# Prompt attention: scores as 64-row products in the two halves of the array, heads inside query tiles

## What is computed

```python
def diff_attention(q, k, v, q_pos, k_pos, lam):
    s = jnp.einsum('bqhcd,bkhcd->bhcqk', q.astype(F32), k.astype(F32)) * (A_HEAD_DIM ** -0.5)
    visible = (k_pos[None, :] // CHUNK) <= (q_pos[:, None] // CHUNK)
    s = jnp.where(visible, s, -jnp.inf)
    p = jax.nn.softmax(s, axis=-1)
    w = p[:, :, 0] - lam * p[:, :, 1]
    return jnp.einsum('bhqk,bkhe->bqhe', w, v.astype(F32))
```

## Time and profile before

| | |
|---|---|
| median of three timed runs | 3132.71 us |
| lowest and highest | 3132.15 and 3134.53 us |
| profiled execution, first to last instruction | 3130.3 us |
| prompt attention in it, first score to last output copy | 1095.0 to 1613.9 us |
| busy in the whole span: PE, DVE, ACT, POOL | 91%, 49%, 33%, 14% |

### The profile page before, as it was taken

One profiled execution on the slowest core, in us unless ns is written; L12 is line 12 of the kernel. 1 busy time (PEld: TensorE's weight loads), 2 busy tenths in 40 slices (PEclk: granted clock), 3 DMA queues, 4 the chain that ended last, 5 costly groups with the idle time before them and its releaser, 6 DMA issues. The chain is left out here.

```text
span 3130.3 us, 41253 instructions
## 1 busy us (share of the span) xinstructions
PE 2847.6 (91%) x12609; PEld 1768.4 (56%) x12610; DVE 1540.2 (49%) x3077; ACT 1025.9 (33%) x2269; POOL 430.3 (14%) x684
## 2 busy tenths in 40 slices
PE   8999999999999688989877999599999999999960
PEld 6777777777777546556555555344444444444430
DVE  2555556555555677877743555422323233232327
ACT  2333333333342255656634555101011111101108
POOL 2111111111111111212210010101110101111000
PEclk9999999999999899999988999699999999999985
DMA  6000100000010240000033222287776557675658
GB/s 233 34 24 24 40 30 23 35 32 27 23 39 25 81 153 9 10 10 8 10 100 110 92 84 86 89 317 271 260 261 234 200 216 269 229 284 191 233 189 307
DMA packets 180197, 382.80 MB, mean 122 GB/s; under 512 B 13571, under 2 KB 51203, under 8 KB 177937
## 3 DMA queue, kind: packets, MB, share of 16 engines
q1 hardware_dynamic: 165808, 333.76, 29.6%
q0 software_dynamic: 14304, 48.08, 4.0%
HBM read 310.73 MB, written 71.08 MB: 122 GB/s over the span
## 5 line engine op out<-in xcount | busy, mean ns | idle before, releaser
L656 PE MATMUL z_psum<-w_in_sb,hT 128*128 128x512 f32 x1088 | 480.5, 592 | 0.0
L650 PE MATMUL z_psum<-hT,w_in_sb 128*128 128x128 f32 x3264 | 374.4, 276 | 0.8 <-ACT hT L326 0.8
L650 PEld LDWEIGHTS z_psum<-hT,w_in_sb 128*128 128x128 f32 x3264 | 370.2, 193 | 1.7 <-ACT hT L326 1.2
L1016 PE MATMUL score_psum<-att_k,q_by_map 128*128 (+3 forms) x640 | 280.2, 565 | 64.9 <-ACT probs L877 29.4
L1970 PE MATMUL gate_psum<-w_gate_sb,block_rows_T 128*128 x720 | 321.2, 599 | 5.6 <-SPq L1802 3.7
L656 PEld LDWEIGHTS z_psum<-w_in_sb,hT 128*128 128x128 f32 x1088 | 200.5, 190 | 221.0 <-issue 221.0
L1994 PE MATMUL down_psum<-w_down_sb,hidden_T 128*128 x720 | 323.7, 592 | 0.9 <-ACT hidden_T L1876 0.9
L1974 PE MATMUL up_psum<-w_up_sb,block_rows_T 128*128 x720 | 316.3, 592 | 0.0
L877 ACT ACTIVATE probs<-score_psum,neg_max 128x512 f32<-128x512 f32 (+3 forms) x320 | 196.4, 621 | 149.5 <-DVE neg_max L945 148.6
L1679 PE MATMUL y_psum<-w_out_sb,mix_T 128*128 128x512 f32 x544 | 243.6, 601 | 0.9 <-DVE mix_T L1536 0.9
L1974 PEld LDWEIGHTS up_psum<-w_up_sb,block_rows_T 128*128 128x128 f32 x720 | 136.8, 190 | 172.2 <-issue 172.2
(11 more groups left out here) (311 smaller groups left out, 3653.7 us busy)
## 6 DMA issues: line engine op xcount, KB each, us to landing
w_gate_sb<-in_w_e_gate SPq DMA_DIRECT2D x32, 2048.0 KB
w_up_sb<-in_w_e_up SPq DMA_DIRECT2D x32, 2048.0 KB, 15.2
w_down_sb<-in_w_e_down SPq DMA_DIRECT2D x32, 2048.0 KB, 18.2
expert_rows<-scratch_moe SPq DMA_DIRECT2D x17, 1024.0 KB, 8.2
w_in_sb<-in_w_in SPq DMA_DIRECT2D x7, 2048.0 KB, 19.6
scratch_z<-z_ring SPq DMA_DIRECT2D x34, 256.0 KB, 2.0
scratch_h<-h SPq DMA_DIRECT2D x17, 512.0 KB, 2.6
x_tile<-in_x_prompt SPq DMA_DIRECT2D x16, 512.0 KB
```

The lines of the kernel that those rows point to most:

```text
L650: mm = pe.matmul(out[:, hd * P:(hd + 1) * P], w[:, c, col:col + P], hT[:, u, c, :], start=(c == 0), stop=(c == DC - 1))
L656: mm = pe.matmul(out[:, :], hT[:, u, c, :], w[:, c, g * HW:(g + 1) * HW], start=(c == 0), stop=(c == DC - 1))
L1016: mm = pe.matmul(sps[(BASE[i] + s) % 2][:, c, 0:kw * P], qz[:, i % 2, c, :], k[:, k0:k0 + kw, bass.ds(h * P, P)], start=True, stop=True)
```

## The change

Four things change together.

- The scale of 1/8 moves from `maps` into the copy that takes q out of PSUM in `project`; `q_by_map` and `maps` are gone, and in `attend_sample` two scalings become copies.
- A map's scores are a product over that map's 64 partitions alone, map 0 on rows 0 to 63 of the array, map 1 on rows 64 to 127. A segment of 512 columns stays one product per map; map 0's product stands ahead of map 1's.
- The order is one list of 64 units, tile by tile and in a tile head by head, all written out. The lags stay: `turn` and `weighted` three units later, `out_row` four.
- q, k and v of a group of tiles come in with all heads, one semaphore for the three; outputs of four heads are stored together, 512 columns. PE's wait for its own transposes is gone, ACT waits on `w_ok` and `tg_ps` in its place. Map 0's probabilities keep four buffers, map 1's have two.

```diff
-                    nc.scalar.copy(z[:, j, :], zps[0][:, :]).then_inc(z_act, 1)
+                    nc.scalar.activation(z[:, j, :], zps[0][:, :], ACT.Copy, scale=Q_SCALE if j == QA else 1.0).then_inc(z_act, 1)
...
+    UNITS = [(i, h) for i in range(NT) for h in range(HEADS)]
+    NU = len(UNITS)
+    SEGS = [seg_of(i) for i, h in UNITS]
+    FIRST = [sum(len(s) for s in SEGS[:u]) for u in range(NU + 1)]
+    GROUPS = [0, 1, 2, 4, 8, NT]
+    LAG = 3
...
+                for buf, src in ((k, dr["z"][KT]), (q, dr["z"][QA]), (v, vp)):
+                    sp.dma_start(buf[:, c, :], src[c].rearrange("t p d -> p t d")).then_inc(t_in[g], 16)
+            for i in range(NT):
+                sp.wait_ge(o_ok, HEADS * (i + 1))
+                sp.dma_start(dr["att"][i], o[:, i % 2, :]).then_inc(att_out[i % 2], 16)
...
+            def expo(u, s):
                 if s == 0:
-                    wait(act, wt_tile, h * NT + i - 3)
+                    wait(act, w_ok, FIRST[max(u - 1, 0)])
+                    wait(act, tg_ps, FIRST[max(u - 3, 0)])
...
-            def maps(h, i):
-                wait_loaded(dve, q_in, q_rest, h, i)
-                wait(dve, s_ps, h * PER_HEAD + (BASE[i - 1] if i else -NSEG[NT - 1]))
-                for c in range(2):
-                    r = slice(64 * c, 64 * c + 64)
-                    ins = ts(qz[r, i % 2, c, :], q[r, i, bass.ds(h * P, P)], scale, None, ALU.mult)
-                ins.then_inc(qz_ok, 1)
...
-            def scores(h, i, s):
-                if s == 0:
-                    pe.wait_ge(qz_ok, h * NT + i + 1)
-                    wait_loaded(pe, k_in, k_rest, h, i)
-                pe.wait_ge(e_ok, n + 1)
-                for c in range(2):
-                    mm = pe.matmul(sps[(BASE[i] + s) % 2][:, c, 0:kw * P], qz[:, i % 2, c, :],
-                                   k[:, k0:k0 + kw, bass.ds(h * P, P)], start=True, stop=True)
+            def scores(u, s):
+                if h == 0 and s == 0 and i in GROUPS:
+                    pe.wait_ge(t_in[GROUPS.index(i)], 48)
+                wait(pe, e_ok, n - 1)
+                for c in range(2):
+                    r = slice(64 * c, 64 * c + 64)
+                    mm = pe.matmul(sps[n % 2][:, c, 0:kw * P], q[r, i, head(u)], k[r, k0:k0 + kw, head(u)], start=True, stop=True)
                 mm.then_inc(s_ps, 1)
...
-                if s == NSEG[i] - 1:
-                    pe.wait_ge(tg_ps, n + 1)
-                    pe.sem_inc(wt_tile, 1)
...
+            for u in range(NU + LAG):
+                cur, old = count(u), count(u - LAG)
+                for s in range(max(cur, old)):
+                    if s < old:
+                        turn(u - LAG, s)
+                    if s < cur:
+                        scores(u, s)
+                    if 0 < s < old:
+                        weighted(u - LAG, s - 1)
+                if old:
+                    weighted(u - LAG, old - 1)
```

More of the change, by code:

```diff
@@ L24 @@
 HIDDEN = -1e30
+Q_SCALE = 64 ** -0.5
 DEC_B = 8
@@ L757, in attend, with count, cols, head @@
     ident = consts["ident"]
[L758 to L794, removed]
+    UNITS = [(i, h) for i in range(NT) for h in range(HEADS)]
[4 more added lines that the diff above has]
+    LAG = 3
+    def count(u):
+        return len(SEGS[u]) if 0 <= u < NU else 0
+    def cols(u, s):
+        k0, kw = SEGS[u][s]
+        return slice(k0 * P, (k0 + kw) * P)
+    def head(u):
+        h = UNITS[u][1]
+        return slice(h * P, (h + 1) * P)
     with ExitStack() as ctx:
@@ L886, in factor, with copy_T @@
+                ins.then_inc(e_ok, 1)
+            def factor(u):
+                act.wait_ge(nM_ok, u + 1)
+                for c in range(2):
+                    ins = nc.scalar.activation(fac[:, u % 2, c, 0:count(u)], nmax[:, u % 2, c, 0:count(u)], ACT.Exp,
+                                               scale=-1.0, bias=tot[:, u % 2, c:c + 1])
                 ins.then_inc(ef_ok, 1)
-            def copy_T(h, i, s):
-                n = h * PER_HEAD + BASE[i] + s
-                kw = seg_of(i)[s][1]
+            def copy_T(u, s):
+                n = FIRST[u] + s
+                kw = SEGS[u][s][1]
@@ L986, in step, with out_row @@
+            def out_row(u):
+                i, h = UNITS[u]
+                dve.wait_ge(pv, FIRST[u + 1])
+                if h == 0:
+                    wait(dve, att_out[i % 2], 16 * (i // 2))
+                nc.vector.tensor_copy(o[:, i % 2, head(u)], ops[u % 2][:, 0:P]).then_inc(o_ok, 1)
+            for u in range(NU + LAG + 1):
+                cur, mid = count(u), count(u - 1)
                 if mid:
-                    factors(h1, i1)
+                    factors(u - 1)
                 if cur:
-                    seg_max(h, i, 0)
+                    seg_max(u, 0)
@@ new lines, in turn, with weighted @@
+            def turn(u, s):
+                n = FIRST[u] + s
+                k0, kw = SEGS[u][s]
+                pe.wait_ge(w_ok, n + 1)
+                wait(pe, wt_sb, n - 1)
+                for b in range(kw):
+                    mm = pe.transpose(tps[n % 2][:, b * P:(b + 1) * P], p0[:, u % 4, (k0 + b) * P:(k0 + b + 1) * P], ident[:, :])
+                mm.then_inc(tg_ps, 1)
+            def weighted(u, s):
+                n = FIRST[u] + s
+                k0, kw = SEGS[u][s]
+                if s == 0:
+                    wait(pe, o_ok, u - 1)
@@ L1046, in weighted @@
                 mm.then_inc(pv, 1)
-            def step(h, i):
-                cur = NSEG[i] if i < NT else 0
-                h3, i3, old = tile_before(h, i, 3)
+            for u in range(NU + LAG):
+                cur, old = count(u), count(u - LAG)
                 for s in range(max(cur, old)):
                     if s < old:
-                        turn(h3, i3, s)
+                        turn(u - LAG, s)
                     if s < cur:
-                        scores(h, i, s)
+                        scores(u, s)
```

176 lines of the change are left out of this document (55 added, 121 removed).

## The result

The changed kernel took 3061.89 us (median of 4 runs, 3059.75 to 3064.2) against 3133.62 us before (4 runs, 3132.15 to 3134.7): a ratio of 0.9772, 95% interval 0.976 to 0.9784.

A forecast was written before the change was run, and what follows sets the result against it. No engine was full in prompt attention; a ring of waits among ACT, DVE and PE bound it. Terms -4.4 - 36.8 + 8 + 0.5 = -33 us on 3130.3 gave 3097.5; medians lie 2.4 higher, so 3100, range 3078 to 3124.

The forecast's parts named there:

- Scores: Prompt attention's score products on 64 rows: three passes' time instead of four, plus two shape changes of 0.15 us; -4.4 us.
- The rival that had them side by side: Score products of both maps overlap fully, pass by pass: 3086 us, or 3076 with free shape changes; chance 0.20.
- S: Time a whole segment's scores occupy TensorE in prompt attention: 1.71 us before, forecast 1.58, counted 34 times in all.
- the ring: Prompt attention's cycle of waits: ACT for DVE's maxima (148.6 us), DVE for PE's scores (42.7), PE for exponentials (29.4).
- Heads inside tiles: New order of prompt attention: -36.8 us in tiles 0 to 4, +8 us (0 to 16) for work moved into larger tiles.
- The opening: Tiles 0 to 4 of all four heads, now with light company: forecast 80.8 us against 117.6 before.
- The company in the large tiles: Weighing and transposes moved into larger steps: 1.4 us a head in tiles 12 to 15, 0.6 in 5 to 11.
- The rest: Removed `maps`, scale in q's copy, PE's dropped wait, loads, stores, straight-line code: practically nothing; tail about +0.5 us.
- Nothing coincides: Rival: score passes of the two maps never overlap: 3115 us, or 3125 with dear shape changes; chance 0.18.
- Starved opening: Rival: tiles 0 to 4 lower the granted clock, making TensorE slower there: +11 us, 3111; chance 0.10.
- Slower, by a low clock in the large tiles: Rival: granted clock falls past the small tiles too: 3171 us at 0.75, 3306 at 0.6; chance 0.07.
- Large steps under 11 us: Sign of a wrong forecast: large-tile steps this short would mean scores weighed more in the cycle of engine waits than assumed.

The follow-up runs named there:

- same-half run: Changed kernel with both score products on rows 0 to 63, so map 1 repeats map 0's scores: ratio 1.0417, stage 521.2 us; whole time not comparable.
- run with padded copy and 128 rows: Changed kernel with VectorE's zero-padded copy of q put back and score products over 128 rows: 3087.77 us, ratio 0.9854.
- both undone: Changed kernel with heads outside tiles again and 128-row score products, without the padded copy of q: ratio 1.0334, stage 496.0 us; whole time not comparable.
- full rows: Changed kernel with both score products over all 128 rows, q and k whole: ratio 1.0247, stage 469.4 us; whole time not comparable.

## Why the prediction was wrong

Four of the runs stand between the kernel before and the changed one like the rungs of a ladder, a step for each edit or group of edits. The stage in us, by tiles and for all four heads (windows that end where a copy of an output ends a step, as in the earlier trace rows), and the ratio of the whole time:

| | before | loop written out | + loads, scale, waits, buffers | + heads inside, stores of four heads | + 64 rows | + no padded copy (after) |
|---|---|---|---|---|---|---|
| tiles 0 to 4 | 115.0 | 109.0 | 108.6 | 79.7 | 79.2 | 79.3 |
| 5 to 7 | 78.7 | 75.5 | 75.0 | 66.0 | 65.2 | 65.0 |
| 8 to 11 | 129.4 | 127.6 | 127.7 | 130.2 | 121.2 | 120.6 |
| 12 to 15 | 177.6 | 176.4 | 173.1 | 176.9 | 159.9 | 159.3 |
| tail | 18.1 | 18.2 | 18.5 | 17.8 | 17.9 | 17.9 |
| stage | 518.8 | 506.7 | 502.9 | 470.6 | 443.4 | 442.1 |
| ratio | 1 | 0.9972 | 0.9954 | 0.9854 | 0.977 | 0.9772 |

One profile stands behind each column, so a difference of 1 or 2 us in it says nothing. What a step is worth also depends on those taken before it: 64 rows are worth 27.2 us behind the change of order and 34.3 ahead of it.

*Scores: forecast -4.4, measured -27.* The step that failed is this sentence: "in program order only map 0's second and map 1's first can coincide". In the trace all four do, in two pairs, the two of a pair 0.007 us apart (median of the 109 whole segments of the changed kernel). Since four passes on one half run strictly one behind the other (the same-half run), a pair must be one pass of each map: map 1's half did not wait until map 0's had both its passes. A segment's scores take 1.06 us against 1.719 in 128 rows, 0.66 less where I had 0.13. The rival that had them side by side named the mechanism. Both of us took the turns too low: 0.15 us each, where the same-half run has 0.39 for the two, half of it outside the scores' own passes. With all of it, from the last pass ahead of a segment to the second behind it, the changed kernel takes 1.48 us and the run with padded copy and 128 rows 1.94, 0.46 less. The Trainium skill's sentence that products in different row groups start about 4 ns apart ("TensorE: Matmul & The Clock Gate", Part 3, The mechanism) agrees with the 7 ns here better than what I made of its strict order. The Trainium skill's rule that a change of tiling mode drains the engine ("TensorEngine Tiling (Array Packing)", Key Properties) agrees too: pass starts stand 0.20 us apart at the turn into the scores and 0.52 at the turn out, where without a turn it is 0.11 and 0.43.

How well the weight of S in the ring was forecast stays open. I had 34 times a stage; 27.2 / 0.66 is 41, and with the turns whole 27.2 / 0.46 is 59. The truth may lie between, since the turn into the scores is hidden where these wait for exponentials. In tiles 12 to 15 it is 17.0 us over 16 steps, 1.6 S a step by the first price and 2.3 by the second, where I had 1 to 2. TensorE was nearly full there, 175.2 of 176.9 us. It was so in the old order too (both undone: 41.0 of 43.1 us a head), and there the same edit takes the same 17.0 us off these tiles; the 7 us by which it is worth more in that order lie in tiles 0 to 7.

*Heads inside tiles: forecast -36.8 and +8.* The opening came out at 79.3 us where I had 80.8. But its 117.6 of before was too much by 2.6 (head 1 took 30.0 us, not 32.9), and 6 us of the remaining 35.7 belong to the loop. The order alone took 28.9 off tiles 0 to 4. The company in the large tiles is there, and of the forecast size: +2.5 in tiles 8 to 11 and +3.8 in 12 to 15. The order as a whole gave -32.3 where I had -28.3 with the tail; that these lie close is luck, since the order took less off the opening than I had and something I had not off the middle tiles. What I missed lies in tiles 5 to 7, where the order took off 9.0 us. In the old order each head brought its small tiles, the granted clock fell in each, and tiles 5 to 7 ran at 0.83 to 0.92 with TensorE full; I read the 0.91 of the earlier trace rows as evidence for a fall and did not see that the new order passes through it once. Now the clock is low once, at the start, and 1.00 from tile 5 on. That the clock is the cause there is read from windows; no run held the clock and changed the order. The nearest to it are heads 0 to 2 of the run with both undone, in tiles 5 to 7:

```profile
1118.90:1135.80 16.90, 15.20 (x64) 9.38 (x65) 13.71 (x40) 11.16 (x40) 3.44 (x6) 1.00 0.59 214
1239.70:1258.10 18.40, 17.07 (x65) 10.07 (x66) 13.84 (x40) 11.24 (x40) 3.44 (x6) 0.91 0.04 11
1361.70:1379.20 17.50, 16.84 (x65) 10.46 (x66) 13.83 (x39) 11.26 (x39) 3.44 (x6) 0.90 0.04 13
```

The head at 1.00 is the fastest. In the run with heads outside, whose 64-row products leave TensorE busy 13.2 to 14.5 us, the same tiles take 16.8 to 16.9 us at 0.81 to 0.91: there a low clock cost nothing to speak of.

*The rest: forecast nothing, measured about 17.* Writing out the loop was worth 12.1 us of stage (9 of time). I had argued that head 0 was straight-line and its small steps "were no slower for it", which answers whether the new code would lose, and never asked what the loop cost: 2 us of idle time at a turn, with "issue" as the only releaser. At the two turns into heads 2 and 3 that is some 4 us (step 0 fell from 9.4 and 9.2 us to 7.3 each); the rest of the 12 is spread over the tiles by one to three microseconds, and I can't place it. The loads, waits and buffers gave 3.8. The scale in the copy of q has the duration taken from the earlier trace rows, but on 34 copies and not 17, since k's became an activation too: 34 × 0.012 = 0.4 us, too little to be told:

```profile
L339 ACT ACTIVATE z_ring<-z_psum x34: 597/597/598, 26.1 to 1007.3; 128x512 f32<-128x512 f32 x34
```

`maps` is free in the changed order, as claimed, but cost 6.9 us with heads outside and 128 rows: the cover is that of an order, not of the operation.

*The other rivals.* Nothing coincides: refuted by the pairs. Starved opening: the granted clock was lower than in the earlier trace rows for head 0, 0.71 for 0.75; it fell to 0.50 (1.2 GHz) at 1086.3 us, while TensorE waited 15.4 us for the first tiles, and but for a few microseconds was back at 1.00 (2.4 GHz) from 1140.9. TensorE was busy 51.8 of 79.3 us, and the opening still took less than forecast. With 128 rows the same opening had 0.87 and took 79.7, with more work for TensorE; what the low clock costs there by itself no run shows. Slower, by a low clock in the large tiles: refuted, 1.00. "Large steps under 11 us" was named as the sign of scores that weigh more in the ring than I gave them: tile 15's steps took 10.8 to 11.1, against 12.3 forecast. Twice the 0.52 by which S came out under my 1.58 is 1.0 of the 1.2 to 1.5 us missing, so it was S more than its weight.

## What to carry to other kernels

When a product's contraction is half the array and a second, independent one stands beside it, put them in the two halves back to back and price them as one, plus about two tenths of a microsecond at each turn of the array's shape, half of it on the work ahead or behind; work out what the bound is with that price before assuming that other engines' rings keep the gain. A hardware loop is a cost like any other: look at the idle time that ends on "issue" at its turn, on every engine, before costing "written out" at nothing. Where thin stretches recur, look at the granted clock in the full ones behind each; an order that gathers the thin ones in one place has that fall once.

## What the runs showed of the hardware

Two 32-bit products on different halves of the array run pass by pass beside each other, in pairs 0.007 us apart; their weights load in pairs as well, all four in 0.30 us (the row at 1504.90), where the kernel before shows 0.19 for each one in turn. Two products on the same half run no faster than two on all 128 rows: 0.429 us a pass in both, plus the turns, 0.39 us for the way in and out. The 0.10 us on the first pass is no mark of the turn alone: in the kernel before, with 128 rows throughout, a segment's first pass takes 0.43 us with other work right ahead of it (38 whole segments) and 0.50 to 0.53 where the pass ahead of it had started a quarter of a microsecond or more before (55).

In the opening, where the code is the same but for the shape of the products, the granted clock was 0.71 with two halves (after) and 0.82 with 128 rows (full rows), and with the padded copy 0.65 and 0.87. It was 0.60 over 88.0 us with both products on one half, although TensorE was busy longest there (78.9 us). A lower clock itself lengthens busy time, so these rows don't tell which comes first; the cause of the levels stays open.
